# Choosing table rows two turns ahead, and holding each row gather until the tenth before it has landed

## What is computed

```python
def chunk(xc):                                        # 128 tokens at a time
    q = (xc @ wq).reshape(PEER_CHUNK, PEER_HEADS, 2, half)
    s1 = jnp.einsum('chd,hnd->chn', q[:, :, 0], keys1).astype(jnp.float32)
    s2 = jnp.einsum('chd,hnd->chn', q[:, :, 1], keys2).astype(jnp.float32)
    v1, i1 = lax.top_k(s1, PEER_TOPK)                 # 16 of 128
    v2, i2 = lax.top_k(s2, PEER_TOPK)
    cand = (v1[..., :, None] + v2[..., None, :]).reshape(PEER_CHUNK, PEER_HEADS, PEER_TOPK * PEER_TOPK)
    cidx = (i1[..., :, None] * PEER_N_KEYS + i2[..., None, :]).reshape(PEER_CHUNK, PEER_HEADS, PEER_TOPK * PEER_TOPK)
    best, pos = lax.top_k(cand, PEER_TOPK)
    eidx = jnp.take_along_axis(cidx, pos, axis=-1)
    g = jax.nn.softmax(best, axis=-1)
    a = jnp.einsum('chkd,cd->chk', u_tab[eidx], xc)
    wgt = (jax.nn.gelu(a.astype(jnp.float32)) * g).astype(xc.dtype)
    return jnp.einsum('chk,chkd->cd', wgt, v_tab[eidx])
```

## Time and profile before

| what | value |
|---|---|
| median of three runs | 1843.68 us |
| the profiled execution | 1844.83 us, its span 1842.8 us |
| TensorE busy | 1497.4 us (81%) |
| VectorE busy | 889.1 us (48%) |
| GpSimd busy | 501.4 us (27%), 512 of its instructions are gathers |
| ScalarE busy | 303.8 us (16%) |
| on the chain that ended last | PE 73%, issue 9%, POOL 6%, DMA 5% |

### The profile page before, as it was taken

The page is one execution under the profiler, slowest core; times in us unless marked ns, Lnnn a source line. Parts: engine busy times, 40 slices in busy tenths (PEclk is TensorE's granted clock), DMA queues, the critical chain, the costliest instruction groups (busy, mean ns, idle before and its releaser), DMA issues.

```text
span 1842.8 us, 17400 instructions
## 1 busy us (share of the span) xinstructions
PE 1497.4 (81%) x6106; PEld 826.1 (45%) x6106; DVE 889.1 (48%) x1991; ACT 303.8 (16%) x634; POOL 501.4 (27%) x540
## 2 busy tenths in 40 slices
PE   7999989999999999889999862765858584848376
PEld 6866564443434434575786762322323231313122
DVE  3986143322223232465302774484646556564844
ACT  3113222111101111214201103020202020211001
POOL 3000000000000000000000255657574757575764
PEclk9999989999999999999999976787878786878798
DMA  9649458999999999630134488979897989898996
GB/s 320 246 143 375 163 246 342 427 428 428 429 429 428 429 429 415 223 137 1 58 114 145 148 311 315 371 273 396 303 411 293 397 303 384 301 392 301 388 374 258
DMA packets 135272, 565.35 MB, mean 307 GB/s; under 512 B 11497, under 2 KB 17430, under 8 KB 122732
## 3 DMA queue, kind: packets, MB, share of 16 engines
q1 hardware_dynamic: 60588, 295.66, 40.2%
q0 software_dynamic: 74416, 268.84, 38.3%
q10 hardware_dynamic: 208, 0.09, 0.0%
HBM read 563.49 MB, written 1.06 MB: 306 GB/s over the span
## 4 chain that ended last, share of the span: by engine, by line
PE 73%; issue 9%; POOL 6%; DMA 5%; DVE 3%; another core or an unknown queue 3%; ACT 1%; SPq 0%; DVEq 0%; ACTq 0%
PE psum L405 52%; PE psum L999 20%; POOL ring L1150 6%; DMA ring<-in_ada_w_dram 2%; DMA ring<-in_peer_v_dram,attnT 2%; DMA ring<-in_peer_u_dram,attnT 1%; DVE scratch L2093 1%; DMA arena<-in_hf_w_dram 1%; PE psum L413 0%; PE psum L785 0%; PE psum L791 0%; SPq L1013 0%; PE psum L860 0%; DVE ring L1961 0%
## 5 line engine op out<-in xcount | busy, mean ns | idle before, releaser
L999 PE MATMUL psum<-ring,arena 128*128 128x512 f32 x904 | 440.8, 639 | 268.8 <-DMA ring<-in_peer_v_dram,attnT 140.3
L1150 POOL DMA_INDIRECT ring<-in_peer_u_dram,attnT x251 | 236.1, 941 | 1190.4 <-DVE attnT L2067 1070.7
L999 PEld LDWEIGHTS psum<-ring,arena 128*128 128x128 f32 x904 | 182.0, 204 | 527.1 <-issue 395.7
L2093 DVE CUSTOM_DVE_ANT_0 scratch<-ring,psum 128x1024 f32<-128x1024 f32 x251 | 303.8, 1221 | 86.0 <-DMA ring<-in_peer_u_dram,attnT 57.8
L405 PE MATMUL psum<-ring,arena 128*64 128x512 f32 (+1 forms) x1552 | 343.8, 594 | 1.4 <-DVE arena L1822 1.4
L405 PE MATMUL psum<-actT,ring 128*128 128x256 f32 (+1 forms) x1424 | 269.2, 349 | 28.7 <-issue 26.9
L1150 POOL DMA_INDIRECT ring<-in_peer_v_dram,attnT x256 | 246.6, 963 | 129.3 <-issue 82.6
L405 PEld LDWEIGHTS psum<-actT,ring 128*128 128x128 f32 x1424 | 238.9, 197 | 58.0 <-issue 34.8
L405 PEld LDWEIGHTS psum<-ring,arena 128*64 128x64 f32 (+1 forms) x1552 | 110.5, 137 | 219.2 <-issue 205.8
L1864 DVE TENSOR_TENSOR arena<-arena,psum 128x512 f32<-128x512 f32 x16 | 16.9, 1058 | 203.9 <-PE psum L405 203.9
L1453 ACT ACTIVATE arena<-ident,attnT 128x128 f32<-128x128 f32 x226 | 72.8, 390 | 170.5 <-remote 67.8
(11 more groups left out here) (380 smaller groups left out, 1196.1 us busy)
## 6 DMA issues: line engine op xcount, KB each, us to landing
ring<-in_w_gate_dram SPq DMA_DIRECT2D x32, 2048.0 KB, 12.1
ring<-in_w_up_dram SPq DMA_DIRECT2D x32, 2048.0 KB, 16.5
ring<-in_w_down_dram SPq DMA_DIRECT2D x32, 2048.0 KB, 14.3
ring<-in_w_in_dram SPq DMA_DIRECT2D x15, 2048.0 KB, 14.9
ring<-in_ada_w_dram SPq DMA_DIRECT2D x12, 2048.0 KB, 11.7
ring<-in_w_out_dram SPq DMA_DIRECT2D x4, 2048.0 KB, 8.8
ring<-in_peer_wq_dram SPq DMA_DIRECT2D x4, 2048.0 KB, 10.5
ring<-in_w_attn_out_dram SPq DMA_DIRECT2D x2, 2048.0 KB, 8.9
```

Of the source, the lines that this page charges most:

```text
L999: last = nc.tensor.matmul(psum[:, 4 + 2 * t + n, :], diag[:, i, :], row_buf(b, use)[:, n * 512:(n + 1) * 512], start=first, stop=final)
L1150: pool.indirect_dma_start(out=row_buf(b, use), out_offset=None, in_=tab, in_offset=bass.IndirectOffsetOnAxis(ap=rowid[:, j // 4, k:k + 1], ...
L2093: V.tensor_tensor_reduce(dotjunk[:, i % 2, :], row_buf(b, use), x, 1.0, 0.0, ALU.mult, ALU.add, dots[:, t, k:k + 1]).then_inc(ev("dotted"), 1)
```

## The change

`picks_of(2)` is called right after `weigh(0)`, and in turn j the call is for `picks_of(j + 2)`. VectorE's order becomes picks 0, picks 1, dots 0, weigh 0, picks 2, dots 1, weigh 1, picks 3, dots 2, ... dots 5, weigh 5, picks 7, dots 6, weigh 6, dots 7, weigh 7. GpSimd's order of gathers stays. Each gather from the eleventh on also waits until the gather ten places ahead of it has landed. Nothing is computed otherwise.

```diff
@@ -246,6 +246,11 @@
             n = TURNS.index((table, j)) * GROUP + i
             return n % ROWBUFS, n // ROWBUFS + 1
 
+        def awaited(n):
+
+            m = n - (10)
+            return None if m < 0 else row_place(*TURNS[m // GROUP], m % GROUP)
+
         def on_vector(j, i):
             return i % 2 == 1 and (j == LAST - 1 or (j == LAST and i < GROUP - 4))
 
@@ -1146,6 +1151,9 @@
                     if n >= ROWBUFS:
                         reader, count = row_reader(n - ROWBUFS)
                         pool.wait_ge(ev(reader), count)
+                    landed_row = awaited(turn * GROUP + i)
+                    if landed_row:
+                        pool.wait_ge(ev(f"row_in{landed_row[0]}"), 16 * landed_row[1])
                     k = GROUP * (j % 4) + i
                     pool.indirect_dma_start(out=row_buf(b, use), out_offset=None, in_=tab,
                                             in_offset=bass.IndirectOffsetOnAxis(ap=rowid[:, j // 4, k:k + 1], axis=0)).then_inc(
@@ -2148,6 +2156,7 @@
             picks_of(1)
             dots_of(0)
             weigh(0)
+            picks_of(2)
             for j in range(1, LAST + 1):
                 dots_of(j)
                 if j == 5:
@@ -2155,8 +2164,8 @@
                 if j == 7:
                     final_norm(0)
                 weigh(j)
-                if j < LAST:
-                    picks_of(j + 1)
+                if j + 2 <= LAST:
+                    picks_of(j + 2)
             add_rows(LAST - 1)
             add_rows(LAST)
             into_residual(1)
```

## The result

The changed kernel takes **1825.56 us** (median of 4 runs, 1822.82 to 1827.60) against 1844.03 us for the kernel before in the same comparison (4 runs): a ratio of 0.9898, 95% interval 0.9866 to 0.9929. That is 18.5 us less, where 29.2 were forecast. The profiled execution took 1825.73 us, its span 1823.9.

What follows compares the result with a forecast made beforehand. Gathers were taken as the floor (82 us a pair possible, about 95.5 taken), stopped by late signals and row-number waits. 29.0 - 7.0 + 3.9 + 3.3 = 29.2 us off 1844.8 gave 1815.6, median 1814.5; range 1792 to 1860.

Steps and rivals of the forecast that it cites:

- the forecast case: Whole kernel: 29.2 us saved, giving 1814.5 us, with own ends of 1804 and about 1835; chance 0.50.
- Row-number waits: GpSimd before u3 to u7: five waits for row numbers go, less the usual gaps, saving 29.0 us.
- What is late next: Gathers of u3 to u7: sums of earlier v rows still late, costing 7.0 us, between 0 and 14.
- The start: Picks 2 between weigh 0 and dots 1, priced 14.8 us: net gain 3.9, or -3.3 with picks 2 at 22.
- The end: v5 loses the picks beside its sums, so its stops near the end shrink: gain 3.3 us, 0 to 6.6.
- Landing wait: Second wait on 502 gathers, ten places back, holds nothing back: 0 us, at most 20.
- ScalarE: ScalarE's 250.6 us of waits for `best_shift` go; its diagonals still wait for sums; costed at nothing.
- A: GpSimd's stops only move; the 29.0 us return as longer stops: 1836.5 us; chance 0.21 together with D.
- B: VectorE becomes the bound if picks exceed 48.5 us: slower, middle 1856 us; chance 0.19.
- D: Landing wait binds through late landing signals, stopping GpSimd 2.9 us per backlog, below 15 us; chance 0.21 together with A.
- C: Much faster, DMA bound: a pair of turns comes near 82 us, time 1769 us; chance 0.10.
- late signals: In the turns, full DMA engines make reports of finished instructions late; a gather stop of some 3 us or more clears them.

Runs made afterwards that it cites:

- e11: The changed kernel itself timed again, in a batch where the kernel before took 1729.83 us: 1727.34 us, ratio 0.9990.
- e1: The changed kernel without the landing wait, picks still two turns ahead: 1814.55 us, ratio 0.9884 to the kernel before.
- e2: The changed kernel with picks back in the old order, keeping the landing wait ten places back: 1841.15 us, ratio 1.0022 to the kernel before.
- e4: The changed kernel with picks 2 put ahead of weigh 0: 1806.25 us, ratio 0.9828 to the kernel before.
- e5: The changed kernel with half the matmuls of each row's sum left out, except in a tile's first and last row: 1814.94 us, ratio 0.9859.
- e7: e2 (old order of picks) with the landing wait twenty places back instead of ten: 1846.45 us, ratio 1.0029 to the kernel before.
- e8: e4 (picks 2 ahead of weigh 0) without the landing wait: 1809.85 us, ratio 0.9833 to the kernel before.
- e3: The changed kernel with the landing wait five places back instead of ten: 1820.33 us, ratio 0.9910 to the kernel before.
- e12: The kernel before, old order of picks, with SyncE's plain loads of consecutive rows replacing GpSimd's gathers from u2 on: 1764.36 us, ratio 0.9571.

## Why the prediction was right, and where its terms were off

The direction, the forecast case and the range were right: faster by more than 0.5%, 1825.56 within 1792 to 1860, between the forecast's own ends of 1804 and 1835. The likeliest time was 11 us too low, and part of the success is luck: at the level of e11 the same change gained 2.5 us of 1729.83, and the prediction had no case for such a level. By its steps:

**Row-number waits, 29.0: right.** No such wait is left from u2 on, and each u turn starts at the usual gap. e1 and e2 show that the whole gain comes from the picks' order.

**What is late next, 7.0 taken from 0 to 14: right in size, for half the reason.** The stops grew by 7.2 us (4.9 in u turns, 1.9 in v turns, 0.4 in u2); with slower issue and small gaps it is 9.3. The doubled stop in u turns came as described (1.94 and 2.47 in u3). I had not foreseen growth in v turns or in issue.

**The start, +3.9 (down to -3.3): wrong, -1.7.** This is the largest miss, 5.6 us. The step that failed is the price of picks 2, 14.8 us "as during picks 1", because TensorE sums nothing then. TensorE did not, but gathers ran and ScalarE issued 22 and more diagonals beside it, and picks 2 took 21.2 us (1131.81 to 1152.98). Row 24 of u1 came at 1154.51, 8.2 later than my 1146.3 and 15.6 later than before. Less the 11.4 of the wait before u2 that is a loss of 4.2, of which shorter stops in v0 and other small gains gave 2.5 back. The bound of 22 us that I had named, and thus -3.3, was the better choice: the trace of before already had picks 2 at that length. e4 shows what the place is worth: picks 2 in the 25 us of idle time ahead of weigh 0 costs nothing, and gives 8 to 13 us.

**The end, +3.3 (0 to 6.6): wrong, -0.5.** In v5 there are no picks beside the sums, and both stops stay:

```profile
1659.61 0.94 POOL L1158 DMA_INDIRECT ring<-in_peer_v_dram,attnT  x1 [3.15 <-remote]
1665.92 0.93 POOL L1158 DMA_INDIRECT ring<-in_peer_v_dram,attnT  x1 [5.37 <-remote]
```

I had reasoned from v6, whose gathers have no stop; but v6 gives only half its rows to TensorE, and e5 shows that this is what removes the stop near the end of a v turn, not the missing picks.

**Landing wait, 0 (up to 20 us): nearly right.** 0.2 to 0.3% as a second wait in the old order (e2, e7), nothing that can be resolved in the new one (e1, e8). Ten back holds nothing; five back does (e3) and pays it back. The working had a slip: with its upper price of 20 us the forecast's low end would have been 1852 and not 1835.

**ScalarE, nothing: right.** The waits for `best_shift` gone, the 179.8 us for sums in their place cost nothing that the ledger shows.

The terms as measured, 29.0 - 9.3 - 1.7 and 0.9 from v6 to the end, give 18.9 us; the -0.5 of v5 is inside the 9.3.

**The rivals.** A asked for pairs of 95 us and stops grown by 29; they grew by 7. B asked for picks over 49 us; picks 4 to 7 took 41 to 45. D asked for DMA releases of GpSimd; there are only splinters of 0.3 us. C, the DMA bound, was not what the change does, but its 82 us a pair is the state to which the kernel goes once late signals are away: 84.5 us in e11, the floor in e12. My evidence against it, picks beside sums with full DMA engines, was not the cause: in e12 picks stand beside sums at 406 GB/s and take 14.5 us.

**The basis of the argument.** I ended with the late signals holding most of a pair's 14 us, more than the row numbers do. That was right, and understated: the row-number waits are themselves a consequence, since they come where late signals stretch picks from 14.5 to over 40 us, and are gone in e12 with the old order and short picks. The page of the kernel before had rows that spoke against full DMA engines as the cause, and I passed over them. They are the busy tenths of TensorE and the rate of the DMA engines in 40 slices of the span:

```profile
PE   7999989999999999889999862765858584848376
...
GB/s 320 246 143 375 163 246 342 427 428 428 429 429 428 429 429 415 223 137 1 58 114 145 148 311 315 371 273 396 303 411 293 397 303 384 301 392 301 388 374 258
```

In the eighth to fifteenth slice (322 to 690 us) SyncE's loads run at 427 to 429 GB/s, faster than any gather, and TensorE is busy nine tenths beside them.

As to the rule weighed in the prediction, 358 GB/s for a core's HBM by the Trainium skill's "DMA: Bandwidth & Descriptors", section "Bandwidth": e11 held 409 GB/s over a whole pair and e12 406 over 534 us, so here it isn't the limit, and the gain from the row numbers was never capped by it. The same section gives the 358 for a core whose HBM domain serves a second streaming core as well; this kernel runs on one core, so the prediction weighed a figure for another case.

## What to carry to other kernels

When many short instructions of one engine take three times their usual time, look for what slows all engines at that moment before reordering them: the reorder gives back 1% where the stretch costs 6%. Before a step is moved, price it by its own length at its place in the trace and not by a sibling in a quieter stretch, and first look for a wait of another engine that it would fill. And time the kernel before anew beside each change, since the same kernel on the same chip can stand at another level, where the gain is a tenth.

## What the runs showed of the hardware that I had not expected

- One kernel had two levels of time: 1837 to 1844 us in four comparisons, 1729.83 us (27 runs, 1727.1 to 1732.1) in one, on a chip that had given 1841.37 in another batch. The difference lies in the stage of GpSimd's gathers: the first gather starts at 1043.46 us in the change's profile and at 1045.50 in e11's, and the end is 94 us apart.
- At the slower level, engines beside GpSimd's gathers issue slowly: single matmuls 1 to 2.5 us apart with nothing to wait for, VectorE's picks 41 to 45 us for 14.5 to 14.7. A stop of the gathers frees them. Plain loads by SyncE at 406 to 409 GB/s don't do it.
- Half the bytes, in 41648 packets for 74416, with the same number of gathers changes nothing of it (picks 42 to 46 us at 209 GB/s).
- A second wait on some 500 gathers costs 4 to 5 us in the old order. It isn't in the gap between gathers, which grew by less than 1 ns.
- Open: what in a session makes the difference, and whether the way in which a gather is issued or its scattered rows delay the others. The Trainium skill, "Runtime: NRT & Kernel Launch", section "Instruction fetch mechanics", says that each engine reads its instructions ahead in blocks through a DMA queue of its own and that this is mostly hidden. A late supply could look like the gaps above, but the trace gives it no support: its instruction queues carry 32 and 32 packets in the change's execution and 32 and 32 in e11, and in the former none stands between 1045 and 1072 us, around TensorE's gaps. A fetch that the trace does not record is not excluded, and no run tests it.
